# Two modulation products from whole rows of the weight, and products without use ahead of three matrix stages

## The chip, the cores and the metric

The kernel runs on one core of one Trainium2 chip. Its time is the device time of one launch in microseconds (us). The kernel before took 2125.36 us (median of 3 runs, 2120.46 to 2126.60). The engines are named as the profile names them: PE (TensorE, matrix products; PEld its weight loads), DVE (VectorE), ACT (ScalarE), POOL (GpSimd) and SP (SyncE, which here only issues DMA transfers).

## The reference

Two transformer blocks over 512 tokens of 1024 values, all in float32. Before anything else, the first block turns one condition vector `c` into six vectors of 1024 values, which shift, scale and gate the two halves of the block:

```python
c_act = jax.nn.silu(c)                       # c: 1 x 1024
mod = c_act @ w_ada[l] + b_ada[l]            # w_ada: 1024 x 6144
shift1, scale1, gate1, shift2, scale2, gate2 = jnp.split(mod, 6, axis=-1)
h = modulate(rms_norm(x, norm_mix[l]), shift1, scale1)
proj = h @ w_in[l]                           # then delta rule and sliding-window attention
x = x + gate1[:, None, :] * mixed
h2 = modulate(rms_norm(x, norm_ffn[l]), shift2, scale2)
ffn = hierarchical_moe(h2, ...)              # 32 experts, 2 of them for a token
x = x + gate2[:, None, :] * ffn
```

`shift1` and `scale1` (the first 2048 columns of `w_ada`) are wanted before the first projection can begin; the other four vectors only after the attention. The second block is a SwiGLU layer (`ffn1`), a mixer (`mix`: dilated attention and a gated recurrence) and another SwiGLU layer (`ffn2`), each with an RMS norm ahead of it.

## The kernel before

Five engine programs run side by side and meet at semaphores: `nxt(engine, name, n)` waits until the semaphore `name` has risen by another n. The order on each engine is the order in which the code is written; nothing is scheduled by a planner.

**Weights.** SP loads slots of 1 MB into a ring of six (`load`, L333); the list `SLOTS` says what stands in a slot. `t_slots` takes 256 columns of all 1024 rows, so a slot is 1024 pieces of 1 KB. PE says with `slots_used` that a slot is free.

**The first modulation** (columns 0 to 2047 of `w_ada`) has its own 8 MB buffer, `ada_w`: eight loads of 256 columns each (`sp_ada1`, L372), six of them ahead of the first ring slot and two behind it. Each 256 columns are one dot product over all 1024 rows. Even blocks go through PE (`pe_ada1_row`, L431: eight products of 1 x 256; ACT copies the row out of PSUM, `act_ada1`, L437; `pe_ada1_cols`, L450, turns it into two columns). Odd blocks are summed on DVE (`dve_ada1`, L473 and L476: eight steps of 128 x 256) and turned by PE as well; the last block is half PE, half DVE. Between them PE turns the normed input tiles (`pe_turn1`, L574). `dve_mod` (L481, L486) adds the bias and sets `mod_ready`; on it wait the last turn (`pe_turn1_last`, L581) and ACT's first step of `act_hT` (L540), and behind those the first projection.

**The second modulation** (columns 2048 to 6143) fills 16 ring slots, `ada2`, and is worked off inside the sliding-window attention (`pe_swa`): 16 attention units, and in each PE does the scores of the unit two ahead (L996), `pe_ada2` of the next slot, the turn of this unit's probabilities (L1005) and the values of the unit before (L1018). `pe_ada2` first turns the row that the unit before left (`pe_ada2_turn`, L514: two products with a 128 x 128 stationary tile) and then does eight products of 32 x 256 (L500), in turn on the four groups of 32 columns of the array, so that 32 rows of PSUM hold the same partial sum; ACT copies 128 x 256 out (L506). The columns gather in bank 7, and `dve_ada2` adds the bias after the attention.

**The boundaries.** Ahead of `ffn1`, `mix` and `ffn2` the four token tiles are normed and turned. For tile t, DVE (`dve_factor`, L3001) writes a diagonal matrix of the scale and sets `xn_ready`; PE multiplies the tile's eight 128 x 128 blocks by it (`pe_xT`, L2839: 8 products, 16 instructions), ACT copies the high part of the result (L2937) and DVE the low part (L3006, `hT_low`). PE's next matrix stage waits for the low parts of all tiles: `mix` for 7 of 8 (`all_low`), `ffn1` and `ffn2` for all, since DVE frees their banks (`ffn_free`) behind its last low part. A float32 product of the kernel shows as two PE instructions in the trace.

Of the kernel before, what the change touches and what calls it, by code (L numbers as in the profile page):

```python
# [17 lines left out]
P = 128  # L18
# [108 lines left out]
def build(nc, a, const_dram, out):  # L127

    ctx = ExitStack()
    with ctx:  # L130
        memory = ctx.enter_context(ExitStack())

        def sb(name, shape, dt=F32):
# [30 lines left out]
            "h2_low": ("g_squares", 1), "w_split": ("g_ready", 1), "w_row_ps": ("g_sums", 1), "w_row": ("w_qT", NPAIR), "iota_wide": ("ada_sums", 4),  # L164
# [11 lines left out]
            "e_window": ("cact_ready", 1), "e_gu": ("columns_ready", 1), "e_sg": ("four_ready", 1), "e_hid": ("g_beta", 129),  # L176
            "e_turned": ("ada_taken", 28), "e_hidT": ("ada_turned", 13), "e_y_ps": ("g_exps", 7), "e_scaled": ("g_normed", 2),
# [4 lines left out]
            "ada_half": ("ada1_taken", 5),  # L182
# [108 lines left out]
        plan("ada2", t_slots(w_ada, 2 * D, 6 * D))  # L291
# [112 lines left out]
        def dve_small(dve):  # L404
# [4 lines left out]
            dve.tensor_reduce(first_of_four, ident[:, 0:P:32], AX_X, ALU.add).then_inc(S("four_ready"), 1)  # L409
# [9 lines left out]
        ada_w = region(6144, 16384, "p (i k n) -> p i k n", i=8, n=256)  # L419
        ada_acc = region(22528, 2048, "p (i n) -> p i n", i=8)  # L420
        ada1_row = region(29680, 256)
        first_of_four = region(29936, 1)

        def pe_ada1_row(pe, i):

            if i == 0:
                nxt(pe, "cact_ready")
            pe.wait_ge(S(f"ada_loaded{i}"), 16)
            last = KD if i < 7 else KD // 2
            for k in range(last):  # L430
                mm = pe.matmul(bank[7][0:1, 0:256], cact[:, k:k + 1], ada_w[:, i, k, :], start=(k == 0),  # L431
                               stop=(k == last - 1))
            mm.then_inc(S("ada1_ps"), 1)

        def act_ada1(act):
            nxt(act, "ada1_ps")
            act.activation(ada1_row[0:1, :], bank[7][0:1, 0:256], ACT.Copy).then_inc(S("ada1_taken"), 1)  # L437

        def pe_ada1_cols(pe, i):

            parts = []
            if i % 2 == 0 or i == 7:
                nxt(pe, "ada1_taken")
                parts.append((ada1_row[0:1, :], one[0:1, :]))
            if i % 2:
                nxt(pe, "ada_sums")
                parts.append((ada_acc[:, i, :], one))
            for j in range(2):
                for n, (left, right) in enumerate(parts):
                    mm = pe.matmul(bank[7][:, 256 + 2 * i + j:257 + 2 * i + j], left[:, j * P:(j + 1) * P], right,  # L450
                                   start=(n == 0), stop=(n == len(parts) - 1))
            return mm

        def pe_ada1(pe):
            for t, (row_block, sums) in enumerate(((0, ()), (2, (1,)), (4, (3,)))):
                pe_ada1_row(pe, row_block)
                pe_turn1(pe, t)
                pe_ada1_cols(pe, row_block)
                for i in sums:
                    pe_ada1_cols(pe, i)  # L460
# [7 lines left out]
        def dve_ada1(dve, i):  # L468
            k0 = 0 if i < 7 else KD // 2
            if i == 1:  # L470
                nxt(dve, "cact_ready")
# [36 lines left out]
        def pe_ada2_turn(pe, u):  # L508
            if u < 0:
                return  # L510
# [3363 lines left out]
```

## Time and profile before

| what | us |
|---|---|
| median of 3 runs | 2125.36 |
| the profiled execution | 2125.04 |
| its span in the profile | 2123.3 |
| PE busy | 2020.9 (95%) |
| DVE, ACT, POOL busy | 924.7, 649.9, 699.7 |

PE is busy nearly throughout, and most of that is the large matrix stages. The time of the profiled execution is 1.7 us longer than its span and 0.3 us shorter than the median. In the timeline a row is a run of equal instructions: its start, its length, the engine, the line, what it writes and reads, how many, and in brackets the idle time just before and what ended it. PEclk is the share of TensorE's full clock that was granted: 1.00 is 2.4 GHz, 0.50 is 1.2 GHz.

### The profile page before, as it was taken

The numbers are of one execution on the slowest core, as the hardware profiler recorded it, in microseconds if no ns is written. First come the engines' busy times: TensorE is split into PE (matmuls) and PEld (weight loads), VectorE is DVE, ScalarE is ACT, GpSimd is POOL, SyncE is SP. The second block draws the span as 40 slices with busy tenths as digits, with TensorE's granted clock in tenths as the row PEclk, the third lists the DMA queues.
The fourth block names the chain that finished last, engine by engine and source line by source line (L and its number), as shares of the span: only waits on it lengthen the run. The fifth ranks groups of instructions, "written<-read, shape, count | busy, mean of one in ns | idle before, by whom it ended". The sixth has DMA issues, their size and how long they took to land.

```text
span 2123.3 us, 28963 instructions
## 1 busy us (share of the span) xinstructions
PE 2020.9 (95%) x11708; PEld 1563.6 (74%) x11708; DVE 924.7 (44%) x1512; ACT 649.9 (31%) x991; POOL 699.7 (33%) x332
## 2 busy tenths in 40 slices
PE   7999989898998979999999899999999999999998
PEld 3887788786444437888888788888568778888887
DVE  4387555555666763323203423338255352232202
ACT  3355523332100123222213324324253342222212
POOL 0333134200222224444443343345034414444432
PEclk8999999999999999999999999999999999999999
DMA  9225500005989971333222322234132232223222
GB/s 316 88 80 164 195 3 3 2 5 228 360 359 417 374 292 60 99 99 99 100 94 85 120 80 80 95 105 129 51 119 96 86 117 77 91 91 98 99 99 89
DMA packets 161389, 278.22 MB, mean 131 GB/s; under 512 B 9847, under 2 KB 131667, under 8 KB 152820
## 3 DMA queue, kind: packets, MB, share of 16 engines
q1 hardware_dynamic: 154800, 267.56, 35.5%
q10 hardware_dynamic: 5092, 4.73, 0.7%
q0 software_dynamic: 1376, 4.26, 0.6%
q8 instruction: 84, 1.38, 0.3%
q14 instruction: 37, 0.30, 0.0%
HBM read 272.28 MB, written 4.24 MB: 130 GB/s over the span
## 4 chain that ended last, share of the span: by engine, by line
PE 83%; DVE 6%; DMA 4%; issue 2%; ACT 2%; SPq 1%; DVEq 1%; POOL 1%; ACTq 0%; POOLq 0%
PE bank L2757 58%; PE bank L2348 6%; PE bank L1274 2%; PE bank L2020 1%; PE bank L3564 1%; PE bank L2362 1%; PE bank L3583 1%; DMA hT<-in_w_up 1%; DMA arena<-in_w_up 1%; PE bank L2368 1%; SPq L372 1%; PE bank L500 1%; PE bank L2369 1%; PE bank L3207 1%; PE bank L3187 1%
## 5 line engine op out<-in xcount | busy, mean ns | idle before, releaser
L2757 PE MATMUL bank<-hT_high_split,ring_split 128*128 128x512 f32 x2496 | 778.8, 391 | 4.6 <-DVEq L2880 3.0
L2757 PEld LDWEIGHTS bank<-hT_high_split,ring_split 128*128 128x128 f32 x2496 | 469.9, 188 | 103.1 <-DVEq L2880 3.5
L2757 PE MATMUL bank<-hT_split,ring_split 128*128 128x512 f32 x1248 | 486.6, 390 | 0.0
L2741 POOL TENSOR_TENSOR ring_split<-ring,ring_split 128x2048 fp32r<-128x2048 f32 x64 | 294.5, 4604 | 402.1 <-ACT ring_split L2712 402.1
L2712 ACT ACTIVATE ring_split<-ring 128x2048 fp32r<-128x2048 f32 x108 | 206.9, 1916 | 612.6 <-DMA ring<-in_ffn_w_up 185.8
L3120 POOL TENSOR_TENSOR ring_split<-ring,ring_split 128x2048 fp32r<-128x2048 f32 x40 | 186.2, 4656 | 315.6 <-ACT ring_split L2712 315.6
L2757 PEld LDWEIGHTS bank<-hT_split,ring_split 128*128 128x128 f32 x1248 | 235.1, 188 | 48.0 <-issue 0.2
L2757 PE MATMUL bank<-ring_split,hid_high_split 128*128 128x512 f32 x848 | 264.6, 393 | 3.9 <-DVE hid_low_split L1538 2.5
L2757 PE MATMUL bank<-ring_split,hid_low_split 128*128 128x512 f32 x576 | 211.1, 391 | 0.8 <-issue 0.8
L2757 PEld LDWEIGHTS bank<-ring_split,hid_high_split 128*128 128x128 f32 x848 | 159.9, 189 | 38.5 <-DVE hid_low_split L1538 2.8
L2885 DVE TENSOR_TENSOR arena<-arena,bank 128x512 f32<-128x512 f32 x44 | 30.2, 687 | 334.6 <-ACT arena L2862 331.2
L2757 PEld LDWEIGHTS bank<-ring_split,hid_low_split 128*128 128x128 f32 x576 | 108.5, 189 | 23.7 <-issue 1.2
L2439 POOL TENSOR_TENSOR places_moe<-arena,places_moe 128x512 fp32r<-128x512 f32 x32 | 51.8, 1637 | 190.6 <-ACT places_moe L2429 190.6
L2348 PE MATMUL bank<-ring,arena 128*64 128x512 f32 (+2 forms) x272 | 77.2, 646 | 9.7 <-DMA ring<-in_w_up 6.2
L3012 DVE TENSOR_SCALAR arena<-arena 128x1024 f32<-128x1024 f32 x2 | 5.2, 2619 | 185.4 <-DMA constants<-in_mix_norm_pre 93.4
L2888 DVE CAST hid_high_split<-arena 128x512 f32 (+1 forms) x44 | 80.3, 1825 | 6.9 <-issue 6.4
L2497 DVE TENSOR_TENSOR residual<-residual,bank 128x512 f32<-128x512 f32 x128 | 79.4, 681 | 3.9 <-PE bank L2369 3.9
L2757 PE MATMUL bank<-hid_low_split,ring_split 128*128 128x512 f32 x224 | 77.3, 390 | 0.3 <-DVE hid_high_split L3669 0.3
L2348 PE MATMUL bank<-arena 128*32 128x512 f32 (+2 forms) x128 | 63.1, 650 | 11.5 <-DMA hT<-in_w_up 9.3
L2348 PE MATMUL bank<-hT,arena 128*32 128x512 f32 (+2 forms) x128 | 63.2, 651 | 0.0
L2368 PE MATMUL bank<-places_moe,h_low_moe 128*128 128x512 f32 x128 | 57.0, 445 | 3.6 <-POOL places_moe L2439 3.6
L1730 POOL TENSOR_TENSOR arena<-arena,constants 128x256 f32<-128x256 f32 x40 | 31.1, 791 | 86.9 <-PE bank L1274 50.5
(500 smaller groups left out, 2854.2 us busy)
## 6 DMA issues: line engine op xcount, KB each, us to landing
ring<-in_w_in SPq DMA_DIRECT2D x45, 1024.0 KB, 5.0
ring<-in_ffn_w_gate SPq DMA_DIRECT2D x22, 1024.0 KB, 5.2
ring<-in_ffn_w_up SPq DMA_DIRECT2D x22, 1024.0 KB, 5.2
ring<-in_ffn_w_down SPq DMA_DIRECT2D x22, 1024.0 KB, 4.9
ring<-in_w_gate SPq DMA_DIRECT2D x17, 1024.0 KB, 9.6
ring<-in_w_up SPq DMA_DIRECT2D x17, 1024.0 KB, 11.7
ring<-in_w_down SPq DMA_DIRECT2D x17, 1024.0 KB, 13.3
ring<-in_w_ada SPq DMA_DIRECT2D x16, 1024.0 KB, 11.6
```

The lines of the kernel that those rows point to most:

```text
L1274: mm = pe.matmul(dst[rc, j * CHUNK:(j + 1) * CHUNK], left[rc, j, :], right[rc, j, :], start=True, stop=True)
L1730: pool.tensor_tensor(MTl[u % 3], MT[u % 2], four(con(f"level{LEVELS[n]}")), ALU.mult)\
L2348: mm = pe.matmul(dst[c, :].rearrange("p (u n) -> p u n", u=2), left[:, k, c], w[g][:, :, k, :], start=(k == 0), stop=(k == KD - 1))
L2368: pe.matmul(dst, left, y_high[half], start=True, stop=False)
L2439: return pool.tensor_tensor(y_low[half], y_scaled[half], y_high[half].bitcast(F32), ALU.subtract)
L2497: return dve.tensor_tensor(X[:, t, c], X[:, t, c], src[:, :], ALU.add)
L2712: act.activation(high(n), raw(n), ACT.Copy).then_inc(S(f"{tag}_high"), 1)
L2741: pool.tensor_tensor(low(n), raw(n), high(n).bitcast(F32), ALU.subtract).then_inc(S(f"{tag}_low"), 1)
L2757: mm = pe.matmul(dst, left[l], right[r], start=start and n == 0, stop=stop and n == 2)
L2885: dve.tensor_tensor(hid, f_sg[:, u % 2, :], bank[2 * (u % 3) + 1][:, :], ALU.mult)
L2888: dve.tensor_copy(at[0], hid)
L3120: pool.tensor_tensor(low(n), raw(n), high(n).bitcast(F32), ALU.subtract).then_inc(S("mix_low"), 1)
```

## The change

Three things.

**First modulation.** The eight loads are now slabs of 128 rows and 2048 columns, so each partition gets one piece of 8 KB. For each slab PE does four products of 32 x 512, one on each group of 32 columns of the array, summed over the eight slabs in bank 7. One ACT copy of 128 x 512 and four products with the columns 0, 32, 64, 96 of the identity then give all 16 columns at once. DVE's sums are gone.

**Second modulation.** The 16 slots are slabs of the same shape, eight for each half of the 4096 columns. Each unit does four products of 32 x 512. The copy out of PSUM (two of 128 x 256) and the four turning products come once after slab 7 (in unit 10, into free columns of bank 0) and once after slab 15 (before unit 15's turn).

**Boundaries.** Before the turn of the last tile PE waits for the low parts of tile 0 and then does 12 products of the identity with itself into bank 0, whose result nobody reads.

```diff
-        plan("ada2", t_slots(w_ada, 2 * D, 6 * D))
+        plan("ada2", [w_ada[k * P:(k + 1) * P, c:c + 2 * D].rearrange("(k p) n -> p k n", p=P)
+                     for c in (2 * D, 4 * D) for k in range(KD)])
 ...
-                sp.dma_start(ada_w[:, i], w_ada[:, 256 * i:256 * i + 256].rearrange("(k p) n -> p k n", p=P))\
-                  .then_inc(S(f"ada_loaded{i}"), 16)
+                sp.dma_start(ada_w[:, i], w_ada[i * P:(i + 1) * P, 0:2 * D]).then_inc(S(f"ada_loaded{i}"), 16)
 ...
+        def pe_ada_rows(pe, w, k):
+            for g in range(4):
+                mm = pe.matmul(bank[7][32 * g:32 * g + 32, :], cact[:, k:k + 1].broadcast_to([P, 32]),
+                               w[:, 512 * g:512 * g + 512], start=(k == 0), stop=(k == KD - 1))
+            return mm
+        def pe_ada_columns(pe, dst, row_of):
+            for c in range(4):
+                mm = pe.matmul(dst[:, c:16:4], row_of(c), ident[:, 0:P:32], start=True, stop=True)
+            return mm
+        def pe_ada1(pe):
+            nxt(pe, "cact_ready")
+            for k in range(KD):
+                pe.wait_ge(S(f"ada_loaded{k}"), 16)
+                mm = pe_ada_rows(pe, ada_w[:, k], k)
+                if k == 0:
+                    mm.then_inc(S("ada_sums"), 1)
+                if k < NT:
+                    pe_turn1(pe, k)
             mm.then_inc(S("ada1_ps"), 1)
+            nxt(pe, "ada1_taken")
+            pe_ada_columns(pe, bank[7][:, 0:16], lambda c: ada1_row[:, c * P:(c + 1) * P]).then_inc(S("ada1_ps"), 1)
 ...
         def pe_ada2(pe, u):
-            pe_ada2_turn(pe, u - 1)
+            if u == KD:
+                nxt(pe, "ada_taken")
             s = FIRST["ada2"] + u
             need(pe, s)
-            for k in range(KD):
-                g = slice(32 * (k % 4), 32 * (k % 4) + 32)
-                mm = pe.matmul(bank[7][g, 0:256], cact[:, k:k + 1].broadcast_to([P, 32]), w[:, k, :],
-                               start=(k < 4), stop=(k >= 4))
+            pe_ada_rows(pe, ring[:, s % RING, :], u % KD).then_inc(S("slots_used"), 1)
         def act_ada2(act, u):
+            if u % KD == KD - 1:
+                act.wait_ge(S("slots_used"), FIRST["ada2"] + u + 1)
+                for i in range(2):
+                    act.activation(ada_row[i], bank[7][:, 256 * i:256 * i + 256], ACT.Copy)
+                act.drain().then_inc(S("ada_taken"), 1)
 ...
+                if u == AT_SCORES:          # 10
+                    pe_ada2_turn(pe, bank[0][:, 256:272])
 ...
+        def pe_xT_last(pe):
+            nxt(pe, "hT_low", 2)
+            for _ in range(12):
+                pe.matmul(bank[0][:, 0:P], ident, ident, start=True, stop=True)
+            pe_xT(pe, NT - 1)
         def all_low(pe):
-            nxt(pe, "hT_low", 2 * NT - 1)
+            nxt(pe, "hT_low", 2 * NT - 3)
 ...
             act_bias_store(act)
-            for i in range(3):
-                act_ada1(act)
             nxt(act, "brow_stored", 48)
+            nxt(act, "ada_sums")
             act_p1(act, 0)
-            for i in range(2):
-                act_ada1(act)
+            act_ada1(act)
 ...
-            for i in (1, 3, 5):
-                dve_ada1(dve, i)
             p1_low(dve, 0, "p1_low_dve")
-            dve_ada1(dve, 7)
-            nxt(dve, "ada1_ps", 6)
+            nxt(dve, "ada1_ps", 2)
```

Where PE stands before the first projection, it has, before the change, the tail of four row products, two turned input tiles and the columns of single blocks (L574 and L581 turn the input, L450 makes columns):

```order
L450 MATMUL bank<-constants,arena 128x1 x4
L574 MATMUL bank<-constants,arena 128x128 x7
L450 MATMUL bank<-constants,arena 128x1 x2
L431 MATMUL bank<-arena,cact 1x256 x8
L450 MATMUL bank<-constants,arena 128x1 x2
L431 MATMUL bank<-arena,cact 1x256 x4
L450 MATMUL bank<-constants,arena 128x1 x4
L581 MATMUL bank<-constants,arena 128x128 x4
```

With the change PE stands there as follows (L424 is `pe_ada_rows`, L431 now `pe_ada_columns`, L536 and L543 turn the input):

```order
L424 MATMUL bank<-arena,cact 32x512 x4
L536 MATMUL bank<-constants,arena 128x128 x7
L424 MATMUL bank<-arena,cact 32x512 x16
L431 MATMUL bank<-constants,arena 128x4 x4
L543 MATMUL bank<-constants,arena 128x128 x4
```

The last slab's four products are followed by one copy and one set of columns only; before, the last two blocks were each followed by their own.

One unit of the attention on PE, with the scores at its head, before the change:

```order
L996 MATMUL bank<-hT 128x256 x2
L514 MATMUL bank<-arena 128x1 x2
L500 MATMUL bank<-ring,cact 32x256 x8
L1005 MATMUL bank<-constants,arena 128x128 x4
L1018 MATMUL bank<-arena 128x64 x4
```

and unit 10's head, a unit and the next unit's scores with the change (L960 scores, L969 turn, L982 values):

```order
L431 MATMUL bank<-constants,arena 128x4 x4
L960 MATMUL bank<-hT 128x256 x2
L424 MATMUL bank<-ring,cact 32x512 x4
L969 MATMUL bank<-constants,arena 128x128 x4
L982 MATMUL bank<-arena 128x64 x4
```

The two turning products of each unit are gone; four come in one unit of 16 and four at the end.

At the boundary between `ffn1` and `mix`, the end of PE's work with the change (L2807 is `pe_xT`, L2815 the products without use, L2725 the matrix stages):

```order
L2725 MATMUL bank<-ring_split,hid_low_split 128x512
L2807 MATMUL bank<-rms_diags,hT 128x128 x8
L2807 MATMUL bank<-rms_diags,arena 128x128 x8
L2815 MATMUL bank<-constants 128x128 x12
L2807 MATMUL bank<-rms_diags,hT 128x128 x8
L2725 MATMUL bank<-hT_high_split,ring_split 128x512
```

Before, the row of L2815 is missing and the rest is the same.

## Rows read from the trace of the kernel before

**Rows 1.** The page: the chain that ended last, by engine.
```profile
PE 83%; DVE 6%; DMA 4%; issue 2%; ACT 2%; SPq 1%; DVEq 1%; POOL 1%; ACTq 0%; POOLq 0%
```
**Rows 2.** Stretches: busy of PE, PEld, DVE, ACT, POOL; PEclk; DMA share; GB/s.
```profile
0.00:47.75 47.75, 34.95 (x144) 15.19 (x144) 21.42 (x46) 12.00 (x22) 0.21 (x5) 0.93 0.97 312
191.50:246.00 54.50, 53.30 (x549) 38.07 (x549) 33.79 (x93) 38.86 (x133) 14.68 (x16) 1.00 0.97 322
```
**Rows 3.** Timeline of all engines, end of the first modulation.
```profile
36.36 6.21 PE L431 MATMUL bank<-arena,cact 128*1 128x256 f32 x16 [1.91 <-DMA arena<-in_w_ada]
...
39.24 0.35 DVE L473 TENSOR_SCALAR arena<-arena,cact 128x256 f32<-128x256 f32 x1 [1.59 <-DMA arena<-in_w_ada]
...
42.60 0.37 ACT L437 ACTIVATE arena<-bank 1x256 f32<-1x256 f32 x1 [7.28 <-PE bank L431]
...
43.56 1.89 PE L431 MATMUL bank<-arena,cact 128*1 128x256 f32 x8
...
45.91 1.31 PE L450 MATMUL bank<-constants,arena 1*128 1x1 f32 x8 [0.46 <-ACT arena L437]
47.26 0.17 DVE L481 TENSOR_TENSOR mod<-bank,cols 128x16 f32<-128x16 f32 x1 [5.98 <-PE bank L450]
...
47.75 0.78 ACT L540 ACTIVATE hT<-bank,mod 128x512 f32<-128x512 f32 x1 [1.89 <-DVEq L488]
```
**Rows 4.** Stretches with loads in 1 KB pieces, then in 4 KB pieces.
```profile
15.00:29.00 14.00, 14.00 (x69) 6.70 (x68) 12.40 (x27) 3.94 (x11) 0.00 (x0) 1.00 1.10 351
...
232.20:237.00 4.80, 4.80 (x50) 3.68 (x47) 2.59 (x8) 3.26 (x12) 0.00 (x0) 1.00 1.01 396
```
**Rows 5.** Timeline of PE, the first stall of the attention, then one unit.
```profile
196.50 0.44 PE L1005 MATMUL bank<-constants,arena 128*128 128x128 f32 x2 [0.98 <-ACTq L1092]
...
219.38 0.70 PE L996 MATMUL bank<-hT 64*128 64x256 f32 x4
...
220.01 0.61 PE L514 MATMUL bank<-arena 128*128 128x1 f32 x4
...
220.54 1.07 PE L500 MATMUL bank<-ring,cact 128*32 128x256 f32 x16
...
222.97 0.70 PE L996 MATMUL bank<-hT 64*128 64x256 f32 x4
```
**Rows 6.** Timeline of PE in the experts: products on four column groups.
```profile
779.94 0.60 PE L2362 MATMUL bank<-arena 128*32 128x512 f32 x2
...
780.37 0.60 PE L2362 MATMUL bank<-arena 128*32 128x512 f32 x2
```
**Rows 7.** Timeline at the boundaries to ffn1, mix and ffn2.
```profile
802.59 2.05 PE L2839 MATMUL bank<-rms_diags,hT 128*128 128x128 f32 x16 [0.79 <-DVE rms_diags L3001]
...
806.15 0.50 PE L2757 MATMUL bank<-hT_high_split,ring_split 128*128 128x512 f32 x1 [1.51 <-DVEq L2880]
...
1175.82 3.78 PE L2839 MATMUL bank<-rms_diags,hT 128*128 128x128 f32 x16 [3.85 <-DVE rms_diags L3001]
1177.93 0.60 ACT L2937 ACTIVATE hT_high_split<-bank 128x512 fp32r<-128x512 f32 x1 [2.67 <-PE bank L2839]
...
1179.30 0.79 PE L2757 MATMUL bank<-hT_high_split,ring_split 128*128 128x512 f32 x1
...
1750.88 3.05 PE L2839 MATMUL bank<-rms_diags,hT 128*128 128x128 f32 x16 [3.85 <-DVE rms_diags L3001]
...
1755.45 0.79 PE L2757 MATMUL bank<-hT_high_split,ring_split 128*128 128x512 f32 x1 [1.51 <-DVEq L2880]
```
**Rows 8.** Stretches at the boundaries: columns as in rows 2.
```profile
799.50:806.00 6.50, 4.10 (x32) 3.72 (x32) 5.63 (x11) 3.19 (x6) 0.00 (x0) 1.00 0.01 4
1172.00:1174.80 2.80, 0.00 (x0) 0.00 (x0) 2.71 (x5) 1.96 (x6) 0.00 (x0) 1.00 1.09 352
1174.90:1181.60 6.70, 5.78 (x21) 5.31 (x22) 3.53 (x8) 1.55 (x3) 0.00 (x0) 0.50 0.23 63
1751.80:1758.50 6.70, 5.19 (x18) 4.31 (x17) 1.60 (x3) 5.09 (x5) 2.06 (x1) 0.50 0.00 1
```

More of the change, by code:

```diff
@@ L414, in act_c @@
             act.activation(cact[:, :], cols1[:, at:at + n], ACT.Silu).then_inc(S("cact_ready"), 1)
[L419 to L432, printed above, removed]
+        ada_w = region(6144, KD * 2 * D, "p (k n) -> p k n", k=KD)
@@ L435, in act_ada1 @@
         def act_ada1(act):
             nxt(act, "ada1_ps")
[L437 to L460, printed above, removed]
-            pe_turn1(pe, NT - 1)
-            pe_ada1_cols(pe, 5)
-            pe_ada1_row(pe, 6)
-            pe_ada1_cols(pe, 6)
-            pe_ada1_row(pe, 7)
-            pe_ada1_cols(pe, 7).then_inc(S("ada1_ps"), 1)
@@ L468, in dve_ada1 @@
[L468 to L471, printed above, removed]
-            dve.wait_ge(S(f"ada_loaded{i}"), 16)
-            dve.tensor_scalar(ada_acc[:, i], ada_w[:, i, k0], cact[:, k0:k0 + 1], None, ALU.mult)
-            for k in range(k0 + 1, KD):
-                dve.drain()
-                mm = dve.scalar_tensor_tensor(ada_acc[:, i], ada_w[:, i, k], cact[:, k:k + 1], ada_acc[:, i],
-                                              ALU.mult, ALU.add)
-            mm.then_inc(S("ada_sums"), 1)
+            act.activation(ada1_row, bank[7][:, :], ACT.Copy).then_inc(S("ada1_taken"), 1)
@@ L490, in pe_ada2, with pe_ada2_turn @@
         def pe_ada2(pe, u):
[L492 removed]
+            if u == KD:
+                nxt(pe, "ada_taken")
             s = FIRST["ada2"] + u
             need(pe, s)
[L495 to L517 removed]
+            pe_ada_rows(pe, ring[:, s % RING, :], u % KD).then_inc(S("slots_used"), 1)
+        def act_ada2(act, u):
+            if u % KD == KD - 1:
[3 more added lines that the diff above has]
+                act.drain().then_inc(S("ada_taken"), 1)
+        AT_SCORES = 10
+        def pe_ada2_turn(pe, dst):
+            return pe_ada_columns(pe, dst, lambda c: ada_row[c // 2][:, c % 2 * P:c % 2 * P + P])
         def dve_ada2(dve):
             nxt(dve, "ada_turned")
[L521 removed]
+            dve_mod(dve, 32, 48, bank[7][:, 0:16])
         def act_norm(act, junk):
@@ L856, in build @@
         sk3 = skv[:, :, 0:128]
-        ada_row = sm(800, 256)
+        ada_row = [region(at, 256) for at in (25936, 26448)]
         squares_q = region(3072, 2048, "p (t n) -> p t n", t=NT)
@@ L1052, in dve_swa @@
                 nxt(dve, "w_scores")
+                if u == AT_SCORES:
+                    dve.tensor_tensor(mod[:, 16:32], bank[0][:, 256:272], cols1[:, 16:32], ALU.add)
                 if u >= 3:
@@ L2414, in pe_moe @@
                 to_tokens(N_GROUP - 1, t)
-            for t in range(NT):
+            for t in range(NT - 1):
                 pe_xT(pe, t)
+            pe_xT_last(pe)
         def halves(half):
@@ L3801, in _ @@
             pe_ffn(pe, "ffn1")
-            for t in (2, 3):
-                pe_xT(pe, t)
+            pe_xT(pe, 2)
+            pe_xT_last(pe)
             pe_mix(pe)
-            for t in (2, 3):
-                pe_xT(pe, t)
+            pe_xT(pe, 2)
+            pe_xT_last(pe)
             all_low(pe)
```

29 lines of the change are left out of this document (8 added, 21 removed), and 2 rows, old and new, of the table SUCCESSOR.

## The prediction, made before the changed kernel ran

> **What bounds the kernel now.** I read the page's chain first: it runs over PE for 83% of the span, DMA for 4%, everything else in single per cents [rows 1]. So a saving counts where PE itself gets shorter, or where PE stands still. The change touches three kinds of place, and I read each from its own stretch.
>
> *The start.* Until 47.75 us the chain is DMA and then a small series of steps: the DMA engines are 97% busy at 312 GB/s, PE does odd work in 34.95 of 47.75 us [rows 2]. The timeline shows the end. PE waits for the seventh load until 36.36, DVE for the eighth until 39.24. From there on nothing waits for data: PE's seventh row takes 6.21 us, ACT copies at 42.60, PE does the half row from 43.56 (1.89), the last columns at 45.91 (1.31), DVE adds the bias at 47.26, and at 47.75 ACT starts on the first projection's input [rows 3]. 8.5 us lie between the last load and that start.
>
> *The attention.* From 191.5 to 246 PE is busy in 53.3 of 54.5 us, ACT in 38.9, DVE in 33.8 [rows 2]. The DMA engines are full as well (0.97), so both PE and DMA could set the pace. One unit lasts from one pair of scores to the next, 222.97 - 219.38 = 3.59 us; the turning products take 220.54 - 220.01 = 0.53 of it, and no row of the unit has an idle time before it on PE [rows 5]. PE sets the pace.
>
> *The boundaries.* Before the last tile's turn PE is idle for 3.85 us at the ones to `mix` and `ffn2`, 0.79 at the one to `ffn1` [rows 7]. At the first two the granted clock is at its lower level, 1.2 GHz, from about 1174.9 and 1751.8 on, for 6.7 us each; at the one to `ffn1` it stays at 2.4 GHz over idle times of 0.79 and 1.51 us [rows 7, 8].
>
> **Start: the loads.** The bytes are the same, only in pieces of 8 KB in place of 1 KB. With 1 KB pieces the engines move 351 GB/s, with 4 KB pieces 396 [rows 4]. A load of 1,048,576 bytes takes 2.99 us by the first and 2.65 by the second. 8 KB pieces from this weight are not in the trace; the bounds are 2.99 (no gain) and a little under 2.65, and I take the nearest row, 2.65. Eight loads save 8 x 0.34 = 2.7 us, so the last lands at 39.2 - 2.7 = 36.5 (bounds 39.2 and 35.5).
>
> The Trainium skill, "DMA: Bandwidth & Descriptors", section Specifications, gives about 358 GB/s as what one core can draw from HBM. By that figure a load would take no less than 2.93 us and this term would be 0.5 us. The 396 GB/s of rows 4 are above it, so here the row decides; what follows from the rule is a rival below.
>
> **Start: behind the last load.** Four products of 32 x 512, two instructions each, on four column groups. The experts have such products: the next round on the four groups starts 780.37 - 779.94 = 0.43 us later, one instruction lasts 0.60 [rows 6]. Two rounds are 0.43 + 0.60 = 1.0 us at full clock, about 1.9 at half. Half is likely: behind the turn of tile 3 PE has some 1 us of work for each load, and nothing while the first projection slot lands between slabs 5 and 6. Then the copy of 128 x 512 (0.60, the ACT row of that shape [rows 7]), the columns (eight instructions with 128 x 128 weights, 1.31 as at 45.91), and DVE's 47.75 - 47.26 = 0.49 [rows 3]. With 0.15 for three hand-overs: 1.9 + 0.6 + 1.3 + 0.5 + 0.15 = 4.45, so the input stage starts at 36.5 + 4.45 = 40.95. **Saved: 47.75 - 40.95 = 6.8 us.** Bounds: no faster load and half clock 4.1; load at 35.5 and 3.4 us of steps 8.85. DVE's sums and ACT's four small copies go too, which frees nothing on the path: DVE only waited at the end (5.98 us at 47.26 [rows 3]). ACT's new wait, for slab 0's products ahead of the first split of a weight slot, is over long before that slot has landed. The projection's weights, constants and rows queue behind the slabs on the same DMA queue and move forward with them.
>
> **Attention.** Sixteen turning steps of 0.53 go: 8.5 us. Two sets of four products come back, each twice the 0.53: 2.1. The other products cost what they did: before, eight of 256 columns, now four of 512, the same columns on each of the four groups (two rounds of 0.43 against 1.07 for the sixteen instructions [rows 5, 6]). At the first turn PE waits 0.98 us for ACT [rows 5], since ACT first has to copy the first unit's row out; that copy is gone, and I count 0.7 of the wait. **Saved: 8.5 - 2.1 + 0.7 = 7.1 us.** What is late next: a unit of 3.06 us meets ACT's 38.86 / 16 = 2.4 and DVE's 33.79 / 16 = 2.1 us a unit [rows 2], both still shorter (ACT loses its copies besides), and a load of 2.65, or 2.99 at the old rate. If that cover fails the term shrinks towards nothing. PE's new wait at unit 8 for ACT's copy has unit 6's turn, unit 5's values and unit 9's scores ahead of it, some 1.5 us for 0.8 us of copies; I price it at nothing. Bounds 1 and 8.5.
>
> **Boundary to `ffn1`.** The twelve products are 24 instructions of the kind of the tile turns (128 x 128 weights, 128 columns), of which 16 take 2.05 us at full clock [rows 7]: start to start about 0.117, so 2.8 us. PE idles there for only 0.79 us. The turn of tile 3 and all behind it (ACT's copy, DVE's low part, the release of the banks, the first product at 806.15) are late by 2.8 - 0.8 = 2.0, and the clock was at 2.4 GHz already. **Lost: 2.0 us.** Bounds 0 (another overlap) and 2.3.
>
> **Boundaries to `mix` and `ffn2`.** Here 2.8 us fit into 3.85, and the wait for tile 0's low parts is long over. The idle time shrinks to about 1.05 us, which is within what the clock stood through before `ffn1`. If it stays up, at `mix`: the turn takes 2.05 in place of 3.78, its first half is out some 0.9 us sooner (ACT took it at 1177.93), so the stage starts at 1178.4 and not at 1179.30; and the stage's products from 1179.30 to 1181.6 ran at half clock, 2.4 us that give back 1.2. Together 2.1. At `ffn2`, which waits for both halves: 3.05 - 2.05 = 1.0, and 1755.45 to 1758.5 at half clock gives back 1.55, together 2.55 [rows 7, 8]. **Saved: 4.65 us.** Bounds: 0 and 5.
>
> **Sum.** 6.8 + 7.1 - 2.0 + 4.65 = 16.55 us. On the profiled execution's own 2125.04 that is 2108.5; the median of the runs is 0.3 us above that execution, less than I can resolve. What lies between the touched places is PE in a row or chains that begin when PE releases them, so I carry the savings through in full. About 0.3% (6.4 us) is what a measurement of this kernel can tell from no change.
>
> **Rivals.**
> 1. *The clock drops all the same.* A pause of 1.05 us, the turn, and another wait for ACT and DVE may still be too little work for the clock. For it: it was lost at both places. Against it: it stood through 0.79 and 1.51 us before `ffn1` [rows 7, 8]. Then 4.65 is gone: 2113.1.
> 2. *The attention has another bound.* If ACT's chain of exponentials or the loads hold the unit near its 3.59 us, only about 1 of 7.1 us is left: 2114.6. For it: DMA share 0.97; against it: the sums of ACT and DVE above.
> 3. *Large pieces load no faster.* The last load stays at 39.2, the start saves 4.1: 2111.2. Against it: 396 GB/s [rows 4]. The HBM figure of the Trainium skill named above says the same; the trace does not bear it out.
> 4. *Something downstream takes the saving back*, such as the experts' loads, whose stretches with a waiting PE may fall otherwise against the clock's drops. The loss would have to be 10 us or more to bring it within 0.3%: about 2120.
> 5. *Slower: the four groups do not run side by side.* One mechanism, in `pe_ada_rows`: four products share their stationary column and stream four different stretches of 512 columns; were they to run one after another, a slab would take 8 x 0.43 = 3.4 us and not 1.0. That is 2.5 us more in 16 units, 40, and some 7 at the start: 2108.5 + 47 = 2156. It decides as soon as less than two groups overlap. Against it: the old products on the same groups, sixteen in 1.07 us [rows 5], and the experts' of the same width [rows 6].
>
> **How the numbers follow.** The forecast, 2108.5, gets 0.68; rival 1 gets 0.11, rival 2 0.07, rival 3 0.05, rival 4 0.05, rival 5 0.04. The terms' own bounds move the forecast by about 6 us either way. The range of 2100 to 2118 holds the forecast and rivals 1 to 3 with their scatter, and leaves out rivals 4 and 5 and the tails. Faster by more than 0.3% means under 2118.7: the forecast and rivals 1 to 3 nearly in full, less a little for their tails, 0.88. Within 0.3%: rival 4 and those tails, 0.08. Slower: rival 5, 0.04.
>
> **What would show it.** Start: the eighth slab landed by 36 to 37 us, ACT's first input step at 40 to 42, three small steps between. Attention: units of about 3.05 us on PE without idle time, its end some 14 us earlier on the clock of the trace (both savings together). Boundaries: the twelve products in one block of 2.8 us; before `ffn1` PE starts the last turn late and without idle time, before `mix` and `ffn2` with about 1 us of it and a granted clock of 1.00 from the turn into the stage. The prediction is wrong if the products of a slab take over 2 us at full clock, if PE waits for loads or for ACT in the attention, or if the clock falls at those two boundaries.

## The result and the profile after

The changed kernel takes **2109.61 us**, median of 5 runs (2108.15 to 2110.77). The kernel before takes 2125.36 on the same chip, 5 runs (2120.46 to 2126.97). The ratio is 0.9929 with a 95% interval from 0.9918 to 0.9941, so some 15.1 us are saved (12.5 to 17.4). The profiled executions stand at 2108.8 and 2125.04, 16.2 us apart; what follows is read from these two.

The total alone tells little. This table measures each stretch between two events that both traces have (the first or the last instruction of a stage on PE; the first line ends at ACT's first input step, the last one with the last busy instruction; a boundary begins with the last expert product or the turn of tile 0).

```
stretch (us)                                 before    after   change   predicted
start to the input step                       47.75    38.81    -8.94     -6.8
first projection and its turns               143.78   143.47    -0.31      0
attention                                     56.39    49.29    -7.10     -7.1
delta rule, up to the output projection      211.16   214.09    +2.93      0
output projection, router, experts           331.41   331.41     0.00      0
boundary to ffn1                              15.67    18.77    +3.10     +2.0
ffn1                                         354.66   354.63    -0.03      0
boundary to mix                               18.49    17.58    -0.91     -0.9
mix                                          556.56   553.85    -2.71     -1.2
boundary to ffn2                              19.59    18.59    -1.00     -1.0
ffn2 and the end                             364.76   363.42    -1.34     -1.55
sum                                         2120.20  2103.93   -16.27    -16.55
```

The page's chain is PE's as it was [rows 1]:

```profile
PE 84%; DVE 5%; DMA 4%; ACT 2%; issue 2%; SPq 1%; DVEq 1%; POOL 1%; ACTq 1%; POOLq 0%
```

Stretches of the trace after, with the columns of [rows 2]: the start, the middle of the slab loads, the attention, the delta rule.

```profile
0.00:38.81 38.81, 23.45 (x108) 8.18 (x108) 8.50 (x17) 10.75 (x17) 0.21 (x5) 0.91 0.93 360
15.00:26.00 11.00, 9.70 (x59) 4.34 (x52) 4.80 (x11) 2.97 (x7) 0.00 (x0) 1.00 1.01 418
182.28:231.58 49.30, 48.34 (x391) 29.32 (x392) 33.72 (x94) 36.09 (x122) 14.65 (x16) 1.00 0.87 351
231.58:445.67 214.09, 191.47 (x3097) 169.16 (x3097) 113.88 (x241) 63.18 (x123) 59.82 (x68) 0.95 0.02 3
```

The loads run at 418 GB/s, above both rows of [rows 4]. The attention has PE busy in 48.34 of 49.30 us, and the DMA share went from 0.97 to 0.87.

The timeline behind the last slabs answers to [rows 3] (start, duration, engine, line, operation, in brackets the idle time ahead of it and its releaser).

```profile
31.28 1.24 PE L424 MATMUL bank<-arena,cact 128*32 128x512 f32 x8 [3.15 <-DMA arena<-in_w_ada]
...
33.77 1.93 PE L424 MATMUL bank<-arena,cact 128*32 128x512 f32 x8 [1.25 <-DMA arena<-in_w_ada]
...
35.77 0.60 ACT L449 ACTIVATE arena<-bank 128x512 f32<-128x512 f32 x1 [5.00 <-PE bank L424]
...
36.42 1.87 PE L431 MATMUL bank<-constants,arena 128*128 128x4 f32 x8 [0.72 <-ACT arena L449]
38.32 0.17 DVE L452 TENSOR_TENSOR mod<-bank,cols 128x16 f32<-128x16 f32 x1 [5.23 <-PE bank L431]
...
38.81 0.78 ACT L502 ACTIVATE hT<-bank,mod 128x512 f32<-128x512 f32 x1 [2.45 <-DVEq L459]
...
186.51 0.44 PE L969 MATMUL bank<-constants,arena 128*128 128x128 f32 x2 [0.82 <-ACTq L1059]
...
213.22 1.06 PE L424 MATMUL bank<-ring,cact 128*32 128x512 f32 x8
...
216.27 1.06 PE L424 MATMUL bank<-ring,cact 128*32 128x512 f32 x8
```

The last three rows are of the attention: the first turn, where PE still waits 0.82 us for ACT, and a unit, 216.27 - 213.22 = 3.05 us where it was 3.59 [rows 5]. Four products on four column groups, eight instructions, take 1.06 us there, and 1.93 at half clock behind slab 7 (the granted clock is down from 32.0 to 45.8 us).

The boundaries, answering to [rows 7]:

```profile
786.02 3.79 PE L2807 MATMUL bank<-rms_diags,arena 128*128 128x128 f32 x16 [1.47 <-DVE rms_diags L2976]
...
788.52 0.29 DVE L2976 TENSOR_SCALAR rms_diags<-constants,ss_rstd 128x128 f32<-128x128 f32 x1
...
789.60 2.95 PE L2815 MATMUL bank<-constants 128*128 128x128 f32 x24
...
792.38 1.95 PE L2807 MATMUL bank<-rms_diags,hT 128*128 128x128 f32 x16
...
795.85 0.50 PE L2725 MATMUL bank<-hT_high_split,ring_split 128*128 128x512 f32 x1 [1.51 <-DVEq L2855]
...
1161.48 2.84 PE L2815 MATMUL bank<-constants 128*128 128x128 f32 x24
...
1165.49 2.05 PE L2807 MATMUL bank<-rms_diags,hT 128*128 128x128 f32 x16 [1.17 <-DVE rms_diags L2976]
...
1732.93 2.84 PE L2815 MATMUL bank<-constants 128*128 128x128 f32 x24
...
1736.94 2.05 PE L2807 MATMUL bank<-rms_diags,hT 128*128 128x128 f32 x16 [1.17 <-DVE rms_diags L2976]
```

At `mix` and `ffn2` the twelve products lie in PE's wait, 1.17 us of it is left, and the turn takes 2.05 us. At `ffn1` the scale of tile 3 is ready at 788.52 + 0.29 = 788.81, PE comes to the end of tile 2's turn only at 789.6, and the products stand between that and the last turn. The stretches behind the pauses, with the columns of [rows 8]:

```profile
1165.40:1168.10 2.70, 2.09 (x17) 1.90 (x17) 1.93 (x4) 1.12 (x2) 0.00 (x0) 1.00 0.03 9
1168.10:1175.00 6.90, 6.90 (x31) 5.70 (x32) 2.69 (x3) 5.35 (x6) 3.24 (x1) 1.00 0.57 162
1736.90:1740.50 3.60, 2.05 (x16) 1.86 (x16) 2.56 (x4) 2.07 (x3) 0.00 (x0) 1.00 0.00 1
1740.50:1747.00 6.50, 6.50 (x29) 5.38 (x30) 0.00 (x0) 4.13 (x3) 5.49 (x2) 1.00 0.01 3
```

The granted clock is 1.00 from the turn into the stage at both, where it was 0.50.

Behind the first products of `mix` PE waits for DVE before it goes on; first before, then after the change:

```profile
1198.59 0.50 PE L2757 MATMUL bank<-hT_high_split,ring_split 128*128 128x512 f32 x1 [1.56 <-DVE arena L3409]
```

```profile
1186.91 0.50 PE L2725 MATMUL bank<-hT_high_split,ring_split 128*128 128x512 f32 x1 [2.24 <-DVE arena L3384]
```

### The profile page after: what moved, and what is told of

It reads as the page before. It is cut to its first block, busy times and chain, and to the rows that moved or that the text cites. A ratio compares the mean times of both kernels' runs of the same rounds, so it can differ in the third digit from the quotient of the medians.

```text
span 2107.0 us, 28614 instructions
## 1 busy us (share of the span) xinstructions
PE 2008.0 (95%) x11568; PEld 1554.4 (74%) x11568; DVE 908.8 (43%) x1484; ACT 646.4 (31%) x975; POOL 699.0 (33%) x332
## 4 chain that ended last, share of the span: by engine, by line
PE 84%; DVE 5%; DMA 4%; ACT 2%; issue 2%; SPq 1%; DVEq 1%; POOL 1%; ACTq 1%; POOLq 0%
PE bank L2725 59%; PE bank L2315 6%; PE bank L1241 2%; PE bank L1987 1%; PE bank L2329 1%; PE bank L3539 1%; PE bank L3558 1%; DMA hT<-in_w_up 1%; DMA arena<-in_w_up 1%; DMA arena<-in_w_ada 1%; PE bank L424 1%; PE bank L2335 1%; PE bank L3182 1%; PE bank L2336 1%; PE bank L3162 1%
## 5 line engine op out<-in xcount | busy, mean ns | idle before, releaser
L2725 PE MATMUL bank<-hT_high_split,ring_split 128*128 128x512 f32 x2496 | 777.1, 390 | 5.8 <-DVEq L2855 3.0
L2725 PEld LDWEIGHTS bank<-hT_high_split,ring_split 128*128 128x128 f32 x2496 | 468.7, 188 | 103.5 <-DVEq L2855 3.4
L2725 PE MATMUL bank<-hT_split,ring_split 128*128 128x512 f32 x1248 | 485.6, 389 | 0.0
L2725 PEld LDWEIGHTS bank<-hT_split,ring_split 128*128 128x128 f32 x1248 | 234.4, 188 | 48.2 <-issue 0.2
L2725 PE MATMUL bank<-ring_split,hid_high_split 128*128 128x512 f32 x848 | 264.6, 393 | 4.0 <-DVE hid_low_split L1505 2.5
L2725 PE MATMUL bank<-ring_split,hid_low_split 128*128 128x512 f32 x576 | 210.9, 391 | 0.8 <-issue 0.8
L2725 PEld LDWEIGHTS bank<-ring_split,hid_high_split 128*128 128x128 f32 x848 | 159.8, 189 | 38.8 <-DVE hid_low_split L1505 2.8
L2725 PEld LDWEIGHTS bank<-ring_split,hid_low_split 128*128 128x128 f32 x576 | 108.5, 189 | 23.3 <-issue 1.2
L2725 PE MATMUL bank<-hid_low_split,ring_split 128*128 128x512 f32 x224 | 77.0, 389 | 0.0
```

Of the source, the lines that this page charges most:

```text
L2725: mm = pe.matmul(dst, left[l], right[r], start=start and n == 0, stop=stop and n == 2)
```

## Experiments

Ratios are to the kernel before, run beside each. One kernel's runs scatter by up to 14 us, so a term is judged by its own stretch in the profiled execution, and the median says only whether it fits.

```
kernel           median (lowest to highest), runs      before   ratio, 95% interval
no_products      2113.81 (2109.77 to 2120.80),  6      2126.11  0.9940  0.9918 to 0.9961
two_places       2107.99 (2103.37 to 2109.85),  6      2126.11  0.9907  0.9888 to 0.9926
first_only       2116.40 (2112.99 to 2121.12),  8      2126.11  0.9956  0.9940 to 0.9971
second_only      2116.98 (2109.78 to 2123.69), 12      2126.11  0.9957  0.9943 to 0.9971
kb_pieces        2111.47 (2107.79 to 2111.86),  6      2123.10  0.9936  0.9919 to 0.9954
warm_start       2106.56 (2104.36 to 2109.24),  6      2123.10  0.9914  0.9896 to 0.9933
hold_delta       2101.87 (2098.96 to 2104.31),  6      2123.10  0.9895  0.9877 to 0.9913
all_three        2100.53 (2096.82 to 2104.48),  6      2123.10  0.9887  0.9867 to 0.9906
six_products     2112.03, 1 run                        2126.87
three_products   2108.75, 1 run                        2126.87
```

**first_only** and **second_only**: the kernel before with one of the two modulations changed, old boundaries.

> The kernel before with only the first modulation from slabs. Theory A, as the trace after shows: the input stage starts 8.9 us earlier, at 38.8, and the gain is carried through but for stretches of lower clock that fall elsewhere, up to 3 us either way: 2116.4 with 2113.5 to 2119.5. Theory B, the size of the prediction: 6.8 us, 2118.6. Rival C: something behind it takes the gain back, such as the projections' weights or the attention's loads, 2122 to 2125.

> The kernel before with only the second modulation from slabs. Theory A: PE's unit in the attention goes from 3.59 to 3.05 us and the attention ends 7.1 us earlier, 2118.3, with up to 3 us either way for stretches of lower clock behind it. Rival B: the attention gains less without the earlier start, since its loads (2.5 to 2.65 us each, sixteen of them) then stand closer to PE: idle time before the slabs' products and 2121 to 2123. Rival C: the 3.2 us that the changed kernel loses in the delta rule behind the attention come from this change itself (PE reaches it with other data or buffers late) and not from the clock: then they are here too, with the granted clock as in the kernel before, 2121.5.

`first_only` came out at A's 2116.4: input step at 38.46, last slab landed at 33.59. `second_only` has the attention at 49.29 us, the same as the changed kernel to 0.01, so B falls: the loads were no closer without the earlier start. Its median is 9.1 us under the one before, 2 us more than A's 7.1, but the interval (6.2 to 12.1 us) holds both. Its delta rule took 214.12 us, as C has it, but not with the clock that C asks for (0.95, in the kernel before 0.97; the rows follow `no_products`).

**no_products** and **two_places**: the changed kernel without the products, and without those before `ffn1` alone. The edit before `ffn1`, which both have (`no_products` has the like at the other two boundaries; the counts that `all_low` waits for change with it):

```diff
-            for t in range(NT - 1):
+            for t in range(NT):
                 pe_xT(pe, t)
-            pe_xT_last(pe)
```

> The changed kernel without the twelve products at all three boundaries (each last turn runs as in the kernel before). Theory A, each place is worth what the trace after shows: before ffn1 the products cost about 3 us, which comes back; at mix and ffn2 they gave about 1.5 and 2.4, which is lost, so the sum is about 1 us slower, near 2110.5. Theory B, the terms of the prediction: 2.0 back, 4.65 lost, near 2112.3. Rival C, the clock at mix and ffn2 stays up for other reasons (all of the kernel comes earlier than before, and the drops may simply fall elsewhere): granted clock 1.00 at both places without the products, and about 3 us faster, near 2106.6.

> The changed kernel with the twelve products only before mix and ffn2, none before ffn1. Theory A, the products before ffn1 lie on the path in full, because the turn before them ends after tile 3's scale is ready: 2.8 to 3.3 us faster than the changed kernel, near 2106.6. Theory B, as predicted: 2.0 faster, 2107.6. Rival C: DVE and ACT, not PE, set the start of ffn1, so nothing changes, 2109.6.

Without the products the boundary to `ffn1` takes 15.71 and 15.70 us (18.77 with them), 3.1 back as theory A has it, though not by the products alone: in these two traces tile 2's turn ran at full clock (2.05 us), in the changed kernel at half (3.79). In `two_places` PE waits for DVE again ahead of the last turn:

```profile
789.76 2.05 PE L2806 MATMUL bank<-rms_diags,hT 128*128 128x128 f32 x16 [0.78 <-DVE rms_diags L2975]
...
793.32 0.50 PE L2724 MATMUL bank<-hT_high_split,ring_split 128*128 128x512 f32 x1 [1.51 <-DVEq L2854]
```

`no_products` lost the clock at both later boundaries, so its rival C falls:

```profile
1160.90:1167.70 6.80, 5.53 (x21) 5.14 (x22) 3.89 (x9) 1.92 (x4) 0.00 (x0) 0.50 0.25 67
1747.90:1754.70 6.80, 5.29 (x16) 4.17 (x16) 1.38 (x2) 5.92 (x5) 2.96 (x1) 0.50 0.01 2
```

The boundaries take 18.51 and 19.14 us, and `ffn2` with the end 365.23 where the changed kernel has 363.42. Its median fits A and B alike, and the median of `two_places` its A and B; only the stretch decides there.

**The delta rule.** `no_products` and the changed kernel are the same program up to the experts' end, yet it took 210.86 us in this stretch and the changed kernel 214.09:

```profile
231.06:441.92 210.86, 188.23 (x3096) 165.89 (x3097) 113.91 (x241) 63.06 (x123) 60.29 (x68) 0.97 0.02 3
```

The kernel before, then `second_only`:

```profile
247.92:459.08 211.16, 188.71 (x3096) 166.54 (x3097) 114.48 (x241) 63.01 (x123) 59.75 (x68) 0.97 0.02 3
```

```profile
240.50:454.62 214.12, 191.92 (x3097) 169.41 (x3098) 114.25 (x241) 63.01 (x123) 59.71 (x68) 0.95 0.02 3
```

A mean clock of 0.97 over 211 us is some 13 us at half clock, 0.95 over 214 some 21. Summed from the clock in each of the twelve traces, this time sorts them all: 3.4 us at half clock go with 207.45 us for the stretch (the two kernels with filled waits, below), 13.7 with 210.6 to 211.2 (five traces), 20.5 with 214.0 to 214.3 (five traces).

PE's waits for DVE's chain (1.0 to 2.1 us) agree within 0.1 us in these four traces but for two. One of 1.4 us is 1.7 in the kernel before. Ahead of tile 2's weights it is 1.8 us in every trace with both modulations changed (where it is not filled), and 1.0 in the kernel before, `first_only` and `second_only`. Why stays open; it does not sort the short stretches from the long, since `no_products` is short with 1.8 and `second_only` long with 1.0. What does is after which waits the clock falls. After the change, behind the waits of 1.8 and of 2.0 us:

```profile
339.20:342.60 3.40, 3.40 (x64) 3.34 (x64) 1.69 (x4) 0.59 (x1) 0.00 (x0) 0.51 0.00 0
359.70:366.50 6.80, 6.80 (x87) 6.47 (x88) 1.90 (x5) 1.22 (x2) 0.00 (x0) 0.50 0.01 2
```

In the kernel before it fell there once, behind the second of these:

```profile
376.10:379.50 3.40, 3.40 (x63) 3.40 (x62) 0.82 (x2) 1.22 (x2) 0.00 (x0) 0.51 0.00 0
```

**hold_delta** puts products without use into these waits of `two_places` (`pe_hold(pe, b, n)` does n products of the identity with itself into bank b).

```diff
+            if c == 1 and t < 3:
+                pe.wait_ge(S("g_o_taken"), 2 * t + 1)
+                pe_hold(pe, 7, (4, 4, 8)[t])
             if 2 * t + c:
                 pe.wait_ge(S("g_state"), 2 * t + c)
...
                     pe.wait_ge(S("g_o_taken"), 2 * t)
+                    pe_hold(pe, 7, (0, 4, 7, 6)[t])
                     pe.wait_ge(S("g_state"), 2 * t)
...
+                        if u == 0:
+                            pe_hold(pe, 4, 8)
                         pe.wait_ge(S("g_T1"), u + 1)
```

> The kernel with products at two places, and products without use in the delta rule as well: 4 to 8 of them where PE waits 1.0 to 2.1 us for DVE (before the first turned blocks, before the second values of tiles 0 to 2, before the weights of tiles 1 to 3), 41 in all, into a bank that is free there. Theory A, these waits are where the clock is lost, now after one and now after another: no stretch at half clock from 230 to 400 us, and from the attention's end to the output projection about 207 us, where kernels so far took 210.6 to 214.1; the median 2103 or so. Rival B: the products lie on the path (a wait is shorter than they are, above all where the clock is down): 212 to 216 us there. Rival C: the lower clock there costs little, since DVE sets the pace of the delta rule: 210 to 211 whatever the clock.

```profile
231.76:439.22 207.46, 195.06 (x3180) 172.25 (x3179) 113.67 (x241) 63.02 (x123) 60.23 (x68) 0.99 0.02 3
230.00:400.00 170.00, 157.60 (x3008) 141.04 (x3007) 97.23 (x211) 56.39 (x108) 53.37 (x61) 1.00 0.01 3
```

No half clock from 230 to 400 us, and 207.46 us for the stretch: theory A to half a microsecond. In `all_three` it is 207.45. C fails by 2.5 us, B by 4.5. The median of 2101.87 lies 1 us under theory A's.

**kb_pieces**: each slab by two DMAs of 1 KB pieces.

```diff
-                sp.dma_start(ada_w[:, i], w_ada[i * P:(i + 1) * P, 0:2 * D]).then_inc(S(f"ada_loaded{i}"), 16)
+                for odd in range(2):
+                    out_, in_ = (x.rearrange("p (a b n) -> p b a n", b=2, n=256)[:, odd]
+                                 for x in (ada_w[:, i], w_ada[i * P:(i + 1) * P, 0:2 * D]))
+                    sp.dma_start(out_, in_).then_inc(S(f"ada_loaded{i}"), 16)
```

> The changed kernel with each slab of the first modulation loaded by two DMAs whose rows are pieces of 1 KB (every second piece of the slab each), in place of one DMA with rows of 8 KB; products, copies and order are unchanged. Theory A, the row size sets the load: a slab every 2.99 us in place of 2.49, the last one lands 4 us later, at 37.7, the input stage starts at 42.8 and not 38.8, the kernel takes 4 us more, 2113.6. Theory B, the size that the prediction took: 2.7 us more, 2112.3. Rival C, the row size is of no matter and the earlier landing came from less work on the engines: the slabs still land every 2.5 us, 2109.6.

```profile
15.00:29.00 14.00, 11.89 (x68) 4.93 (x60) 4.89 (x11) 3.03 (x8) 0.00 (x0) 1.00 1.10 351
```

351 GB/s, as in the kernel before [rows 4], a slab every 3.00 us, the last one at 37.95, the input step at 43.04: theory A. The kernel before reaches the same rate with one DMA for each load, so it is the size of the pieces and not the number of DMAs. The median decides nothing here: its interval holds 0 us and 4 us more than the changed kernel. The profiled execution is the fastest of the six, and its delta rule took 210.65 us where the changed kernel's took 214.09.

**warm_start**: turns of tile 3 repeated in PE's waits at the start of `two_places`; **all_three** has these and the products of `hold_delta`.

```diff
+        WARM = {5: 21, 6: 7, 7: 4}
...
+                for n in range(WARM.get(k, 0)):
+                    pe.transpose(bank[n % 7][:, 3 * P:4 * P], xn1[:, 3, n % 7 * P:(n % 7 + 1) * P], ident)
```

> The kernel with products at two places (mix and ffn2), and turns of tile 3 repeated on PE while it waits for slabs 6 and 7 and for ACT's copy (21, 7 and 4 of them). Theory A, the half clock behind the last slab is the price of PE's wait of 3.15 us ahead of slab 6: granted clock 1.00 from 30 to 46 us, slab 7's products 1.06 in place of 1.93, the columns 0.95 in place of 1.87, the input stage at 37.0, the first ten products of the projection 2.0 us less, together 3.8: 2104.2 by the 2108.0 of the kernel with two places. Rival B: ACT's splits of the weights hold the projection, so only the start's 1.8 stays, 2106.2. Rival C: repeated turns do not hold the clock, or it falls later instead, 2108.0.

> Products at mix and ffn2, the repeated turns at the start and the products in the delta rule, in one kernel. Theory A, the gains add: 2108.0 - 3.8 - 5 = 2099. Rival B, the start gains only 1.8 and the delta rule nothing: 2106. Rival C, held clocks at one place only move the drops to the next place with waits: 2107 or 2108 with half-clock stretches as long as before in sum (about 85 us in each profiled execution so far).

```profile
34.94 1.06 PE L424 MATMUL bank<-arena,cact 128*32 128x512 f32 x8 [0.56 <-DMA arena<-in_w_ada]
...
36.73 1.06 PE L431 MATMUL bank<-constants,arena 128*128 128x4 f32 x8
...
38.31 0.78 ACT L506 ACTIVATE hT<-bank,mod 128x512 f32<-128x512 f32 x1 [1.63 <-DVEq L463]
...
42.12 0.69 PE L2728 MATMUL bank<-hid_high_split,hid_low_split 128*128 128x512 f32 x1 [0.53 <-DVE hT_split L531]
```

The clock was held, and the steps behind the last slab took 38.31 - 34.90 = 3.4 us in place of 38.97 - 33.88 = 5.1 in `two_places`. But the last slab came 1.0 later (in `all_three` too; why stays open), PE then waited for DVE and the clock fell at 42.2, so the projection gained nothing (143.61 us against 143.43) and the median did not change beyond the scatter. In size this is rival B, with less than its 1.8; the reason is not B's, since PE waited for DVE (1.67 and 0.53 us) and not for ACT's splits, but that of C: the clock fell later instead. `all_three` has the lowest median of the study, by the products in the delta rule; its interval (to 0.9906) and that of `hold_delta` (to 0.9913) lie below that of the changed kernel (from 0.9918). Its rival C falls: the drops did not move elsewhere in full, since the mean granted clock of the execution is 0.985 in `hold_delta` and 0.986 in `all_three`, and 0.978 to 0.983 in the other ten traces.

**six_products** and **three_products**: `range(12)` made 6 or 3 in `two_places`.

> The kernel with products at two places (mix and ffn2), six of them each in place of twelve: 1.4 us of work, so PE's idle time ahead of the last turn is about 2.5 us and not 1.17. Read from its own stretches, not from the total. Theory A, a pause of that length is already too long, as in the first rival of the prediction: granted clock 0.50 behind both pauses, boundary to mix 18.5 us, to ffn2 19.1 to 19.6, as without products. Rival B, half the work is enough: 17.6 and 18.6 us, granted clock 1.00.

> As the kernel with six, with three products each: 0.7 us of work, idle time about 3.15 us. Theory A: the clock falls at both places, 18.5 and 19.1 to 19.6 us. Rival B: it stays up, 17.6 and 18.6; then the length of the pause is not what decides. Rival C: at one place it falls and at the other not, since where a pause falls against the clock's steps decides by chance.

`three_products` came out as its rival C, and `six_products` between its A and B, in one execution each. With pauses of 2.51 us the clock stayed up at `mix` (17.59 us) and fell at `ffn2` (19.79); with 3.18 it stayed up at `ffn2` (18.59) and fell at `mix`, 1.0 us into the turn, too late to delay the stage (17.60). `six_products`, then `three_products`:

```profile
1161.00:1163.50 2.50, 2.05 (x16) 1.86 (x16) 1.82 (x4) 0.91 (x2) 0.00 (x0) 1.00 0.05 12
1736.70:1746.90 10.20, 8.69 (x28) 7.13 (x27) 1.95 (x3) 6.19 (x5) 5.02 (x2) 0.50 0.01 2
```

```profile
1165.10:1168.50 3.40, 3.40 (x14) 3.08 (x13) 1.59 (x4) 1.19 (x2) 0.00 (x0) 0.50 0.07 16
1736.00:1746.00 10.00, 7.56 (x40) 6.45 (x41) 3.37 (x7) 6.57 (x6) 4.51 (x1) 1.00 0.10 32
```

With all twelve, and 1.17 us of pause left, it stayed up 12 times of 12 (six traces, two boundaries each); without products, with pauses of 3.85 us, it fell 8 times of 8. Between, it went either way.

## Why the prediction was right

The time was forecast at 2108.5 and came out 1.1 us above, but the sum is better than its terms: several were mis-sized and one was missing, and that they nearly cancel is luck.

**Start, mis-sized: 8.9 and not 6.8.** The step was "the bounds are 2.99 (no gain) and a little under 2.65, and I take the nearest row, 2.65". Rows of 8 KB load in 2.49 us (landings from 13.61 to 26.04, five steps), so the value lay beyond the bound from 4 KB. `kb_pieces` ties it to the row size. The last slab landed at 33.72, not 36.5. Of these 2.8 us, 8 x 0.16 = 1.3 are the rate; 1.2 came from the slot between slabs 5 and 6, 2.7 us in place of the 3.9 of the execution before, and the rest from an earlier first slab. The slot's part is not one of the pieces' size: `kb_pieces` has 2.7 there too, and its last slab lands 1.3 us ahead of the 39.2 of the kernel before with the same 1 KB pieces. Why stays open. The steps behind the load took 5.1 against 4.45: half clock was foreseen for the products (1.93 measured, 1.9 assumed), but not for the columns (1.87, assumed 1.31). Rival 3 fell. The Trainium skill has a second sentence on this that I missed: "Perfetto Trace Analysis", section Roofline, says a single core may exceed the 358 GB/s, up to about 435 by its sixteen DMA engines. The 418 GB/s here agree: above the one figure and below the other.

**Attention, right: 7.1, with one part that did not come.** The unit is 3.05 us (3.06 forecast), and every trace with the attention changed has 49.28 or 49.29 us. Rivals 2 and 5 fell: PE waits for no load, and for ACT only at the first turn, and the eight instructions on four groups take 1.06 us. But of the 0.7 us that were counted of the wait at the first turn only 0.16 came (0.82 us left of 0.98): after the change ACT itself waits there for DVE's scores, 2.08 us, so the row copy was not all that held it. The sum holds because the rest came out better, such as the two sets of columns, some 1.75 us and not 2.1.

**Boundary to `ffn1`, mis-sized: 3.1 lost and not 2.0.** The step was "PE idles there for only 0.79 us", subtracted from 2.8. That idle time was not there: tile 2's turn ran at half clock (3.79 us) and ended after the scale was ready, so the products, 2.95 us, lay on the path in full. Ten traces without them have 15.67 to 16.21 us at this boundary, the two with them (this one and `kb_pieces`) 18.77: a price of 2.6 to 3.1. In both of these two tile 2's turn ran at half clock, which the products behind it cannot have caused. Three traces without products (`first_only`, `warm_start`, `all_three`) have that turn at half clock as well, 3.59 us, and 16.07 to 16.09 us; by these 2.7 of the 3.1 us are the products and 0.4 the clock. Whether 2.0 would be right with the turn at full clock no run shows.

**Boundaries to `mix` and `ffn2`, right in the mechanism; `mix` mis-sized: 1.3 and not 2.1.** At `ffn2` 2.55 were predicted and 1.00 + 1.34 measured. At `mix` 0.91 came up to the stage, and its sixth product starts 1.26 us into it where it was 2.30, so the clock gave back 1.0 of the 1.2. But at the 73rd product the wait for DVE is 2.24 us in place of 1.56, and 0.4 is left of it (`two_places`, `kb_pieces` and `hold_delta` show the same). The step was to carry the clock's gain through the stage, past a wait that DVE sets. Rival 1 fell (12 of 12), though with six or three products it would have come true at one place in two. The other 2.3 of the 2.7 us that `mix` got shorter are not the products': 1.5 are a stretch of 3.4 us at half clock at 1509.4 in the execution before, absent after, which is chance, since `two_places` has one at 1496.5; the rest lies mostly at a short wait for DVE at 1657.7 in the execution before.

**"I carry the savings through in full", wrong by 2.9 us.** This step failed, and it is a small form of rival 4: the delta rule lost 2.9, as the clock fell behind other waits of PE. It is no effect of the change's instructions alone, since `no_products` has them and took 210.86. It is not a fixed cost of the earlier start either: with the attention changed, the stretch took 214.0 to 214.3 in the changed kernel, `two_places`, `second_only`, `warm_start` and `three_products`, and 210.6 to 210.9 in `no_products`, `kb_pieces` and `six_products`. The two traces with the old attention (211.2 and 210.6) are too few to tell whether the change makes the long stretch likelier. `hold_delta`, which only fills the waits, takes 207.46: the clock is worth more here than the whole of the 2.9. The Trainium skill, "TensorE: Matmul & The Clock Gate", Part 1, says that the chip's look at PE's activity runs freely and does not begin anew with a kernel; two lengths of the stretch from the same instructions are in keeping with that, but no run here shows it.

## What to carry to other kernels

Read a gain stage by stage between events that both traces share: here the total came out right by errors of +2.1 (start), -2.9 (delta rule), -1.1 (`ffn1`) and +1.5 us (`mix`). Products without use pay where PE waits for longer than they last and the granted clock is lost behind the wait (18.49 to 17.58 us, and 214.1 to 207.5 in the delta rule); where the next operand is ready first they cost nearly their whole length (2.7 of 2.95 us). A saving also moves all that follows against the clock's drops, so a few microseconds of any forecast are chance until the waits are filled.

## What the runs showed of the hardware that was not expected

In the profiled execution of `no_products` PE waited 7.9 us in `mix` where it waits 2.2 in the trace after, and 4.3 us of the difference are one DVE instruction:

```profile
1184.97 4.79 POOL L3094 TENSOR_TENSOR ring_split<-ring,ring_split 128x2048 fp32r<-128x2048 f32 x1 [4.11 <-ACT ring_split L2679]
...
1185.32 4.98 DVE L3066 TENSOR_TENSOR arena<-arena 128x512 f32<-128x512 f32 x1
...
1191.12 0.79 PE L2724 MATMUL bank<-hT_high_split,ring_split 128*128 128x512 f32 x1 [7.89 <-DVE arena L3383]
```

The same DVE instruction takes 0.69 us in the trace after, where it began ahead of POOL's:

```profile
1185.40 0.69 DVE L3067 TENSOR_TENSOR arena<-arena 128x512 f32<-128x512 f32 x1
...
1186.38 4.59 POOL L3095 TENSOR_TENSOR ring_split<-ring,ring_split 128x2048 fp32r<-128x2048 f32 x1 [5.46 <-ACT ring_split L2680]
```

In `no_products` POOL began 0.35 us ahead, and DVE ended 0.5 us behind POOL. A smaller case of it stands in the traces before, after and of `no_products` alike. In the trace after, a DVE instruction on 128 x 8 values takes 4.20 us and ends 0.02 us behind POOL's two; the next on the same shape takes 0.17.

```profile
1171.76 9.17 POOL L3095 TENSOR_TENSOR ring_split<-ring,ring_split 128x2048 fp32r<-128x2048 f32 x2 [12.31 <-ACT ring_split L2680]
...
1176.75 4.20 DVE L1127 TENSOR_TENSOR arena<-arena 128x8 f32<-128x8 f32 x1
...
1181.02 0.17 DVE L1129 TENSOR_TENSOR arena<-arena 128x8 f32<-128x8 f32 x1
```

The Trainium skill, "SBUF — State Buffer", section Who interferes with whom, says that a DVE instruction with two SBUF inputs contends with a GpSimd instruction that reads SBUF, and that the order of issue decides which of the two blocks; these traces agree (4.98 us against 0.69). In `no_products` POOL waits there for ACT's split of a weight slot, and ACT for its load, so the order may turn with the landing of a slot; no run was made to test that.
